# Order of the weight preparation around the exponentials in the second layer's projections

## The reference

```
h = rms_norm(x, norm1_g);  z = h @ w_in
r, k, v, decay/aaa/gate inputs      -> rwkv7_time_mix (a recurrence over the tokens, 8 heads of 64)
q2, k2, v2                          -> norm and rotation of q2 and k2, causal attention, 8 heads
gate_a (1024), gate_b (1024)        -> sigmoid(gate_a) * branch_a + sigmoid(gate_b) * branch_b
```

## Time and profile before

| what | value |
|---|---|
| median of 3 runs | 1495.42 us |
| lowest and highest run | 1494.83 and 1498.4 us |
| the profiled execution's own time | 1497.31 us |
| its span in the trace | 1495.5 us |
| mean granted clock of TensorE | 0.994 |
| busy: TensorE, VectorE, ScalarE, GpSimd | 1396.5, 519.8, 335.7, 81.1 us |

### The profile page before, as it was taken

How to read it: one execution, slowest core, us unless ns; L and a number is a source line. 1 busy time by engine, 2 the same in 40 slices (tenths; PEclk the granted TensorE clock), 3 DMA queues, 4 the chain that set the end, 5 groups by cost and what they waited for, 6 DMA issues and landing times.

```text
span 1495.5 us, 23575 instructions
## 1 busy us (share of the span) xinstructions
PE 1396.5 (93%) x10118; PEld 785.0 (52%) x10118; DVE 519.8 (35%) x919; ACT 335.7 (22%) x494; POOL 81.1 (5%) x41
## 2 busy tenths in 40 slices
PE   8989999999999998999899989996999999999998
PEld 6543333333333333333333333333978988799998
DVE  1763121111211111211121112116679658665666
ACT  0531011000100010100010001003565543345442
POOL 0000000000000000000000000000000050023222
PEclk9999999999999999999999999998999999999999
DMA  9699999999999999999999999995544214255552
GB/s 361 237 395 385 427 426 428 429 428 429 429 428 429 428 428 428 429 428 427 428 427 428 429 428 429 427 428 214 178 145 155 109 46 157 85 173 192 182 196 84
DMA packets 45125, 491.37 MB, mean 329 GB/s; under 512 B 5008, under 2 KB 5520, under 8 KB 13488
## 3 DMA queue, kind: packets, MB, share of 16 engines
q1 hardware_dynamic: 44928, 490.47, 79.8%
q10 hardware_dynamic: 144, 0.13, 0.0%
HBM read 489.53 MB, written 1.05 MB: 328 GB/s over the span
## 4 chain that ended last, share of the span: by engine, by line
PE 63%; DMA 30%; DVE 5%; ACT 2%; issue 1%; POOL 0%; SPq 0%; DVEq 0%; ACTq 0%
DMA ring<-in_w_exp 17%; PE bank L810 15%; PE bank L839 9%; DMA work<-in_w_exp 8%; PE bank L868 7%; PE bank L869 7%; PE bank L870 7%; DMA spare<-in_w_exp 3%; PE bank L768 2%; PE bank L756 2%; PE bank L705 2%; DMA ring<-in_w_lora 1%; PE bank L626 1%; PE bank L656 1%; PE bank L776 1%; ACT spare L1416 1%
## 5 line engine op out<-in xcount | busy, mean ns | idle before, releaser
L810 PE MATMUL bank<-ring,spare 128*64 128x512 f32 x1344 | 302.2, 596 | 25.3 <-DMA ring<-in_w_exp 25.3
L1884 DVE TENSOR_SCALAR work<-bank 128x512 f32<-128x512 f32 x32 | 22.1, 691 | 741.4 <-PE bank L810 741.4
L810 PEld LDWEIGHTS bank<-ring,spare 128*64 128x64 f32 x1344 | 92.8, 136 | 221.0 <-issue 159.8
L870 PE MATMUL bank<-work_parts,ring_parts 128*128 128x256 f32 x648 | 181.6, 280 | 0.0
L868 PE MATMUL bank<-work_parts,ring_parts 128*128 128x256 f32 x624 | 174.8, 280 | 6.8 <-DVE work_parts L1943 4.5
L869 PE MATMUL bank<-work_parts,ring_parts 128*128 128x256 f32 x624 | 175.0, 281 | 0.0
L839 PE MATMUL bank<-ring,spare 128*64 128x512 f32 x672 | 148.8, 595 | 14.7 <-ACT spare L1416 14.7
L1412 ACT ACTIVATE work<-work 128x512 f32<-128x512 f32 x32 | 20.2, 631 | 536.1 <-DVE work L1884 536.1
L810 PE MATMUL bank<-work,spare 128*64 128x512 f32 x576 | 129.7, 595 | 8.3 <-DMA work<-in_w_exp 8.3
L868 PEld LDWEIGHTS bank<-work_parts,ring_parts 128*128 128x128 f32 x624 | 119.3, 191 | 8.5 <-issue 4.8
L870 PEld LDWEIGHTS bank<-work_parts,ring_parts 128*128 128x128 f32 x648 | 123.3, 190 | 0.0
(11 more groups left out here) (420 smaller groups left out, 1649.2 us busy)
## 6 DMA issues: line engine op xcount, KB each, us to landing
ring<-in_w_exp SPq DMA_DIRECT2D x126, 2048.0 KB, 34.6
work<-in_w_exp SPq DMA_DIRECT2D x54, 2048.0 KB, 34.6
spare<-in_w_exp SPq DMA_DIRECT2D x12, 2048.0 KB, 31.6
ring<-in_ffn_up SPq DMA_DIRECT2D x22, 1024.0 KB, 4.8
ring<-in_ffn_down SPq DMA_DIRECT2D x22, 512.0 KB, 3.4
ring<-in_w_in SPq DMA_DIRECT2D x2, 2048.0 KB, 17.1
ring<-in_w_out SPq DMA_DIRECT2D x4, 1024.0 KB, 16.7
ring<-in_w_k SPq DMA_DIRECT2D x4, 1024.0 KB, 5.2
```

The lines of the kernel that those rows point to most:

```text
L810: ins = pe.matmul(to[n2 * CAP:(n2 + 1) * CAP, :], x_e[:, 2 * j + kk, :], w[:, b, kk, n2 * BANK:(n2 + 1) * BANK], start=False, stop=j == UP ...
L870: return pe.matmul(to, left[1], right[0], start=False, stop=stop, skip_group_check=True)
L1884: dve.tensor_scalar(gt, bank[4][:, :], LIMIT, None, ALU.min).then_inc(gt_ready, 1)
```

## The change

Two calls move, nothing else. On ScalarE the cast of `v2`, half 0, moves from behind the three exponentials to ahead of the wait for `cs_ready`. On VectorE the lower part of `gate_a0`, half 1, moves from behind the five operand instructions to directly behind that of half 0, ahead of the wait for `exp3_ready`. The counts of `half_upper` and `half_rest` are reached in the same order as before, and no instruction is added or taken away.

```diff
--- before.py
+++ after.py
@@ -1481,11 +1481,11 @@
                 act.copy(g_gate[:, t, :], bank[2 + t][:, :]).then_inc(lora_up_ready, 1)
             upper("k2", (1,))
 
+            upper("v2", (0,))
             act.wait_ge(cs_ready, 1)
             act.activation(e_pos, cs, ACT.Exp, scale=-KAPPA).then_inc(exp3_ready, 1)
             act.activation(e_neg, cs, ACT.Exp, scale=KAPPA).then_inc(exp3_ready, 1)
             act.activation(e_before, sd, ACT.Exp, scale=-KAPPA).then_inc(exp3_ready, 1)
-            upper("v2", (0,))
 
             def raw_qk(w, f, pair):
 
@@ -2022,14 +2022,13 @@
                 ins = dve.scalar_tensor_tensor(out=kk2[:, i, :], in0=zr[:, i, :], scalar=col2("rwkv_r_k_2")[:, i:i + 1], in1=zk[:, i, :],
                                                op0=ALU.mult, op1=ALU.mult)
             ins.then_inc(rk_ready, 1)
-            rest_half("gate_a0", (0,))
+            rest_half("gate_a0")
             dve.wait_ge(exp3_ready, 3)
             link(dve.tensor_tensor(ar[:, :, 1, :], zr, e_pos, ALU.mult))
             link(dve.scalar_tensor_tensor(out=ar[:, :, 0, :], in0=kk, scalar=-1.0, in1=e_before, op0=ALU.mult, op1=ALU.mult))
             link(dve.tensor_tensor(aa, aa, kk, ALU.mult))
             link(dve.tensor_tensor(b_hat, aa, e_neg, ALU.mult))
             dve.tensor_tensor(k_hat, zk, e_neg, ALU.mult).then_inc(hats_ready, 1)
-            rest_half("gate_a0", (1,))
 
             dve.wait_ge(qkv2_raw, 4)
             heads = lambda a: a.rearrange("p w t (h d) -> p (w t h) d", d=HD)
```

## The result

| | before | after |
|---|---|---|
| median | 1495.36 us (6 runs) | 1502.16 us (6 runs, 1501.05 to 1504.21) |
| profiled execution, own time and span | 1497.31 and 1495.5 us | 1502.92 and 1501.1 us |
| mean granted clock of TensorE | 0.994 | 0.990 |

The ratio is 1.0044, with a 95% interval of 1.0031 to 1.0057: slower by 6.6 us, beyond 0.3%. The prediction was 1498.6, within 1495.4 to 1501.8, at 0.77 for "within 0.3%". The mean clocks of the two profiles don't measure the change: near 110 us, long before it, after has 10.3 us at 0.50 and before 3.4.

The account below looks back on a forecast made before the run. TensorE was taken as the bound. Minus 2.5 us for the removed stall, plus new stalls of 2.0, 1.0 and 2.6, gave about 3.2 late: 1498.6 us against the median 1495.42, range 1495.4 to 1501.8.

Parts of the forecast that it names:

- The transfer lands too late for the cast: ScalarE: `v2`, half 0, lands at 1106.65, so the cast ahead of the exponentials waits until then.
- The table load comes into the open: ScalarE: the exponentials' load runs behind the moved cast, no longer in idle time; first exponential 5.04 us late.
- the row: Profile row of ScalarE's table loads before the change: 1.29 us from load start to next operation, against the skill's 2.66.
- the square roots: ScalarE, line 1499: 3.25 us late, at 1115.07, making VectorE's chain from 1113.01 equally late.
- The stalls: TensorE: new delays of 2.0 us before `v2` half 1, 1.0 before `gate_a0` half 0, 2.6 among line 954's transposes.
- The sum up to `gate_b0`: TensorE: minus 2.5, plus 2.0, 1.0 and 2.6 gives 3.1; by end points `gate_b0` starts 3.2 us late.
- its step: TensorE: 2.5 us won between `gate_a0`'s halves, all but 0.1 to 0.2 given back waiting for the sigmoids.
- the clock falls: Rival, chance 0.12: TensorE's clock drops behind the new stalls, losing 1.7 us per fall; 4.9 late, 1500.3.
- a forecast that kept it at 1.00: Main forecast, chance 0.65: 3.2 us slower, 1498.6, with no PEclk below 1.00 between 1125 and 1190.
- the 2.3 stall of today: TensorE's 2.3 us wait between `gate_a0`'s halves before the change; cited against a clock fall.
- two such, 1502.0: Clock rival with two falls: 6.6 us late, 1502.0.
- the 3.2 stays to the end: Behind 1149.80 everything follows TensorE's rhythm, so the 3.2 us lateness neither grows nor shrinks.

Follow-up runs that it names:

- the first edit alone: Kernel before with only ScalarE's cast of `v2`, half 0, moved ahead of the exponentials: ratio 1.0019.
- the wait filled: Two extra 128x512 matmuls in TensorE's wait among the transposes: on the changed kernel ratio 1.0019, on before with the second edit only 0.9993.
- the second edit: Kernel before with only the lower part of `gate_a0`, half 1, moved ahead of the five operand instructions: ratio 1.0012.
- the table load first: Changed kernel with a one-element exponential ahead of the moved cast, so the table load runs in ScalarE's idle time: ratio 1.0014.
- the three with the sigmoids first: `gate_a0`'s sigmoids, bonus copy moved earlier: on the second edit 0.9992, on the changed kernel 1.0013, on the second edit with `gate_b0` half 1's lower part earlier 0.9994.

## Why the prediction was wrong

**Right, step by step.** The transfer lands too late for the cast: the cast starts at 1106.00, 1106.5 with the offset (forecast 1106.65). The table load comes into the open: 1.28, as the row had it and not 2.66; the exponential starts 4.90 late (5.04), the square roots 3.10 (3.25). That a switch of tables costs a drain on top of the load, as the Trainium skill has it (ScalarE: Activation LUTs, section What ACT_TABLE_LOAD costs), isn't seen here either, and the measurement decides: the load starts 0.01 behind the cast and the exponential 1.30 behind the load's start. The stalls are 1.67, 0.82 and 2.56 of idle time (forecast, as delays, 2.0, 1.0, 2.6), the third for the sigmoids, the fourth group's bonus in time. The sum up to `gate_b0` is 3.1 where the clock holds (3.2), in the first edit alone and with the wait filled. And the second edit is worth nothing by itself once the clock is kept: plus 0.11 with the wait filled, where its step had minus 0.1.

**Wrong: the clock.** The step that failed is the rival "the clock falls" at 0.12, against 0.65 for a forecast that kept it at 1.00. Its reason against, "the 2.3 stall of today, behind dense work, left the clock at 1.00", took one wait in one profile to stand for another. The runs showed in its place: the wait of 2.5 among the transposes brings a fall of 3.4 us at 1.2 GHz that costs 1.6 locally, in three of the four profiles that have it unfilled (not in the one with the table load first). The size was forecast well (1.7), the chance was not. With it alone the sum is 4.7, or 1500.1, inside the range.

**Also wrong: the upper end.** The measured 6.6 and 5.5 lie above 4.7. In both profiles of the changed kernel a second fall, near 1310, adds 1.5; I had it only as "two such, 1502.0", left outside the range, and "the 3.2 stays to the end" left no room for it. By the marks, 3.1 of shift, 1.6 and 1.5 of clock, less 0.2 to 0.6 given back, make the 6.1 and 5.7 of the two profiles, beside 6.6 and 5.5 in the ratios. The second fall is not a sure part of the change: it is missing in the one profile of before and in three others, but it is there in kernels whose clock held near 1150 (table load first, and the three with the sigmoids first). The wait ahead of it is in before and after alike:

```profile
1306.31 0.35 PE L868 MATMUL bank<-work_parts,ring_parts 128*128 128x256 f32 x1 [2.25 <-DVE work_parts L1943]
...
1310.39 0.35 PE L868 MATMUL bank<-work_parts,ring_parts 128*128 128x256 f32 x1 [2.25 <-DVE work_parts L1943]
```

It has this length (2.25 or 2.26) and the same transposes and matmuls on either side in all eleven profiles, and the clock falls at it in seven and not in four. So neither the length of a wait nor the work beside it settles the outcome, and one profile at 1.00 is no reason against a fall; the kernels differ there only in the moment at which the wait comes. What in that moment decides stays open. How often before has that fall in its runs, a single profile can't say, so what part of the 5.5 to 6.6 it carries **stays open**. The comparison is itself uncertain by about 2 us either way.

**The base.** The three runs of before that I saw had the median 1495.42; the six of the first comparison have 1495.36, so there the base isn't why the forecast missed. Later groups have 1496.63, 1496.01 and 1495.88. The spread of the group of 29, 1491.9 to 1500.7, goes for the most part with the mean clock: 1494.1 to 1495.4 at 0.995, 1498.9 to 1499.2 at 0.991, though the slowest run has 0.993. The upper end of the range, 0.4 under the measured median, had no room for that spread.

## What to carry to other kernels

An operation moved into an engine's idle time is free only if its data are there by then and if nothing that was hidden in that idle time, as the table load here, comes into the open: here the idle time was wide enough (8 us), and the wait for the transfer and a load of 1.28 us in the open still made everything behind 3.1 us late. A stall that is taken away must be followed to the next wait in line; if that one is 0.15 us from binding, the stall moves there whole. And where a stall of over 2 us moves or is new, price the clock at even odds, not as an accident, and don't take one profile with the clock at 1.00 for proof: here it fell in 0 of 2, 3 of 4 and 7 of 11 profiles at the three places above. In the wait among the transposes, two matmuls without a use were cheaper than the fall.

## What the runs showed of the hardware

- A wait of TensorE of 2.3 to 2.4 us between two dense halves of a projection left the clock at 1.00 in two of two profiles (before, first edit alone). At a wait of 2.5 to 2.6 us, some 10 us later, behind 16 small matmuls (128 x 2) and 16 transposes, the clock went to 1.2 GHz for 3.4 us in three of four profiles, and TensorE lost 1.6 us.
- At one and the same wait of 2.25 us near 1300 to 1310, with the same work on either side, it fell in seven of eleven profiles, for 3.4 us and a loss of 1.5.
- A table load took 1.28 us and the next function, where its data were there, started 1.29 to 1.30 behind the load's start, in idle time of the engine or in the open. One exponential of a single element ahead of the cast hid the load again, and TensorE was 1.3 us less late.
- Filling such a wait with 1.9 us of matmuls kept the clock at 1.00 behind it in both profiles, and locally the kernels lost 1.6 us less; their ratios fell by 0.18 and 0.19%, which holds the missing second fall too.
- Whole runs of one kernel on this one core differ by up to 8.7 us (before, 29 runs), and mostly the mean granted clock, 0.991 to 0.997, goes with it.
